# Beginning of a two-layer hybrid backbone: x is loaded first, and half of the first modulation rides move in between the chunks of the first feed-forward layer

## The reference

```python
x = x + _pos_2d(L, x.dtype)[None]
mod_lat = (jax.nn.silu(c) @ w_ada[l] + b_ada[l]).reshape(b, N_MOD, D)     # 9 vectors of 1024
mod_ctx = (jax.nn.silu(c_ctx) @ w_ada[l] + b_ada[l]).reshape(1, N_MOD, D)
# _pre:  rmsnorm(x, g) * (1 + mod[3k+1]) + mod[3k]
# _post: x + weight * mod[3k+2] * rmsnorm(y, g)
x  = _post(x,  _swiglu(_pre(x,  g[0], mod_lat, 0), ffn1_gu[l], ffn1_down[l]), g[1], mod_lat, 0, 0.5)
xc = _post(xc, _swiglu(_pre(xc, g[0], mod_ctx, 0), ffn1_gu[l], ffn1_down[l]), g[1], mod_ctx, 0, 0.5)
```

## Time and profile before

| | us |
|---|---|
| median of 3 runs (lowest, highest) | 2723.16 (2721.18, 2723.31) |
| the profiled execution, its own time | 2723.62 |
| its span in the trace | 2721.8 |
| PE busy in the span | 2630.3 (97%) |
| DVE busy | 1659.4 (61%) |
| ACT busy | 716.5 (26%) |
| POOL busy | 819.7 (30%) |

### The profile page before, as it was taken

The page is one execution under the profiler, slowest core; times in us unless marked ns, Lnnn a source line. Parts: engine busy times, 40 slices in busy tenths (PEclk is TensorE's granted clock), DMA queues, the critical chain, the costliest instruction groups (busy, mean ns, idle before and its releaser), DMA issues.

```text
span 2721.8 us, 41131 instructions
## 1 busy us (share of the span) xinstructions
PE 2630.3 (97%) x17188; PEld 2454.1 (90%) x17188; DVE 1659.4 (61%) x2299; ACT 716.5 (26%) x1016; POOL 819.7 (30%) x1286
## 2 busy tenths in 40 slices
PE   5999999998999999999999999999999999999997
PEld 4999999997969899999999899999999868788886
DVE  5788878767663677667666733443334684644444
ACT  5221221223314321111112422122122414422222
POOL 1268867822130200000000148677551051000001
PEclk9999999999999999999999999999999999999999
DMA  9534544453464143443432232222224456233331
GB/s 330 147 113 159 162 140 135 154 176 120 125 181 141 40 132 111 133 128 119 134 119 86 84 87 84 91 86 91 93 92 141 160 160 188 70 93 101 93 93 62
DMA packets 340465, 337.19 MB, mean 124 GB/s; under 512 B 52528, under 2 KB 311224, under 8 KB 336696
## 3 DMA queue, kind: packets, MB, share of 16 engines
q1 hardware_dynamic: 279224, 204.07, 25.4%
q10 hardware_dynamic: 51840, 77.07, 8.5%
q0 software_dynamic: 9216, 53.42, 5.2%
HBM read 290.02 MB, written 44.50 MB: 123 GB/s over the span
## 4 chain that ended last, share of the span: by engine, by line
PE 86%; DVE 9%; ACT 2%; issue 2%; DMA 1%; SPq 0%; DVEq 0%; ACTq 0%
PE ps L462 78%; PE ps L1619 2%; DVE tmpN L1366 1%; DVE xT L1195 1%; PE ps L1644 1%; DVE tmpN L1389 1%; DVE hL L1393 1%; DMA adaW<-in_w_ada_dram 1%; PE ps L1586 1%; PE ps L1230 1%; ACT wH L447 1%; PE ps L1633 1%; DMA xin<-in_x_dram 1%; PE ps L962 1%; PE ps L981 0%
## 5 line engine op out<-in xcount | busy, mean ns | idle before, releaser
L462 PE MATMUL ps<-hH,wH 128*128 128x384 f32 (+1 forms) x2928 | 1012.3, 346 | 6.5 <-DVE hL L1393 3.8
L462 PE MATMUL ps<-hH,wL 128*128 128x384 f32 (+1 forms) x2928 | 1004.1, 343 | 0.0
L462 PE MATMUL ps<-hL,wH 128*128 128x384 f32 (+1 forms) x2928 | 1003.9, 343 | 0.0
L454 DVE TENSOR_TENSOR wL<-raw,wH 128x1024 fp32r<-128x1024 f32 x300 | 389.4, 1310 | 475.5 <-ACT wH L447 473.9
L462 PEld LDWEIGHTS ps<-hH,wH 128*128 128x128 f32 x2928 | 549.5, 188 | 32.1 <-DVE hL L1393 6.2
L462 PEld LDWEIGHTS ps<-hH,wL 128*128 128x128 f32 x2928 | 549.6, 188 | 18.3
L462 PEld LDWEIGHTS ps<-hL,wH 128*128 128x128 f32 x2928 | 549.7, 188 | 17.9
L462 PE MATMUL ps<-midH,wH 128*128 128x384 f32 (+1 forms) x1232 | 424.7, 345 | 3.7 <-DVE yT L874 3.3
L462 PE MATMUL ps<-midH,wL 128*128 128x384 f32 (+1 forms) x1232 | 422.3, 343 | 0.0
L462 PE MATMUL ps<-midL,wH 128*128 128x384 f32 (+1 forms) x1232 | 422.0, 343 | 0.0
L447 ACT ACTIVATE wH<-raw 128x1024 fp32r<-128x1024 f32 x300 | 310.8, 1050 | 421.7 <-PE ps L462 406.8
(11 more groups left out here) (269 smaller groups left out, 2276.6 us busy)
## 6 DMA issues: line engine op xcount, KB each, us to landing
raw<-in_ffn_gu_dram SPq DMA_DIRECT2D x176, 512.0 KB, 3.8
adaW<-in_w_ada_dram ACTq DMA_DIRECT2D x40, 1536.0 KB, 6.9
raw<-in_ffn_down_dram SPq DMA_DIRECT2D x88, 512.0 KB, 3.5
x_d<-xT POOLq DMA_DIRECT2D x4, 3072.0 KB, 10.3
xT<-x_d POOLq DMA_DIRECT2D x4, 3072.0 KB, 11.4
W_d<-gW POOLq DMA_DIRECT2D x16, 512.0 KB, 3.7
VT_d<-gVT ACTq DMA_DIRECT2D x16, 512.0 KB, 3.0
raw<-in_w_in_dram SPq DMA_DIRECT2D x16, 512.0 KB, 4.3
```

Source lines behind the costliest of these rows:

```text
L454: nc.vector.tensor_tensor(wL[:, n % SPLIT_SLOTS, :], raw[:, n % RAW_SLOTS, :], wH[:, n % SPLIT_SLOTS, :].bitcast(f32), ALU.subtract).then_ ...
L462: ins = nc.tensor.matmul(dst, a, b, start=first and n == 0, stop=last and n == 3 * len(pairs) - 1)
```

## The change

Loads: x is issued first on SP. The parameters are divided between SP's queue and ACT's. POOL issues rides 0 to 4 as soon as the context is there, 5 to 7 when xT is complete. All eight rides have buffers of their own now; lt, lamT, modrow and sq_first lie elsewhere.

Start: DVE takes both parts of each chunk from PSUM (the context copies leave ACT), two chunks ahead of the angle reduction and six behind it; ACT squares each chunk as it comes. PE does ride 0 before the sums of squares and rides 1 to 3 behind them. DVE then goes to the coefficients and `pre_vector` straight after the powers k = 2 to 8 and the three wL; cfR, cfI and P8 (now L2287 to L2306) come behind `pre_vector`, and a new semaphore `s_pow` tells ACT and POOL of them. The coefficients are made in three parts: chunks 0 to 3 after four rides, 4 to 6 after five, 7 after six.

First FFN: `first_groups` takes two units and calls `late_rides` after each chunk, which puts rides 4 to 7 and their turns between the chunks. Unit 2 follows alone, then unit 3 as before. The transfers of rides 8 and 9 are issued by ACT in the middle of `add_shift`.

The core of the diff:

```diff
-    def ada_ride(pe, R, bank, col, between=None):
-        pe.wait_ge(ada_first[R % 6], 16 * (R // 6 + 1))
+    def ada_ride(pe, R, bank, col):
+        pe.wait_ge(ada_first[R], 16)
...
+        def late_ride(R):
+            pe.wait_ge(ada_taken, R - 1)
+            ada_ride(pe, R, 4 + R % 2, 0)
+        def late_rides(place):
+            if place == 0:
+                late_ride(4)
+            elif place == 1:
+                ada_turn(pe, 4, 4, 128)
+                late_ride(5)
+            elif place == 2:
+                ada_turn(pe, 5, 5, 128)
+            elif place == 3:
+                late_ride(6)
+            elif place == 4:
+                ada_turn(pe, 6, 4, 128)
+                late_ride(7)
+            elif place == 5:
+                ada_turn(pe, 7, 5, 128)
+        if F.ride0 == FIRST_RIDES:
+            first_groups(pe, F.base, 2, pre, late_rides)
+            pe.wait_ge(ada_taken, FIRST_RIDES)
+            gate_up(2, 2, None)
+        else:
+            first_groups(pe, F.base, 3, pre)
...
+        if F.ride0 == FIRST_RIDES:          # ffn_scalar, before the first gate
+            act.wait_ge(s_pow, 1)
...
+    LATE_COEFS = {4: (5, 7), 7: (6, 8)}
         for m in range(first, KC):
+            if N.after is None and m in LATE_COEFS:
+                dve.wait_ge(ada_taken, LATE_COEFS[m][0])
+                coef_pre(dve, N, m, LATE_COEFS[m][1])
+                dsync(dve)
...
     def start_sync(sp):
+        sp.dma_start(xin[:, 0:2, :], ctx_in[0]...).then_inc(s_xctx, 16)
+        sp.dma_start(xin[:, 2:6, :], x[0]...).then_inc(s_xin, 16)
+        sp.dma_start(prow[8:16, 4, :], c_ctx...).then_inc(s_par, 16)
...
     def start_pool(pool):
         for R in range(FIRST_RIDES):
-            if R == 2:
-                pool.wait_ge(s_xin, 32)
-            if R >= 6:
-                pool.wait_ge(ada_used, R - 5)
-            pool.dma_start(ada_early[R], ada_source(0, R)).then_inc(ada_first[R % 6], 16)
+            if R == 0:
+                pool.wait_ge(s_xctx, 16)
+            elif R == 5:
+                pool.wait_ge(s_xlat, KC)
+            pool.dma_start(ada_early[R], ada_source(0, R)).then_inc(ada_first[R], 16)
...
     def start_scalar(act):
+        act.dma_start(pdt[...], log_dt...) (two), prow <- lam_re, lam_im, norm_g, c
...
-        for R in range(FIRST_RIDES): ...
+        take_rows(act, 0, 0, 0)
+        split_hi(act, 0)
+        take_rows(act, 1, 1, 0)
+        take_turned(act, 0, 4, 0)
+        split_hi(act, 1)
+        take_rows(act, 2, 2, 0)
+        take_turned(act, 1, 5, 0)
+        split_hi(act, 2)
+        take_rows(act, 3, 3, 0)
+        take_turned(act, 2, 4, 128)
+        take_turned(act, 3, 5, 128)
+        add_shift(act, pres[0], 0, 2)
+        take_rows(act, 4, 4, 0)
+        add_shift(act, pres[0], 2, 3)
+        take_turned(act, 4, 4, 128)
+        take_rows(act, 5, 5, 0)
+        add_shift(act, pres[0], 3, 4)
+        take_turned(act, 5, 5, 128)
+        ada_dma(act, FIRST_RIDES)
+        ada_dma(act, FIRST_RIDES + 1)
...
     def start_vector(dve):
+        for n in range(SPLIT_SLOTS):
+            split_lo(dve, n)
+        dve.wait_ge(s_parT, 3)
+        dve.wait_ge(ada_taken, START_RIDES)
+        coef_pre(dve, pres[0], 0, 4)
+        pre_vector(dve, pres[0])
+        make_fold(dve, FIRST_RIDES)
         lr, li = lamT[:, 0, 0:64], lamT[:, 0, 64:128]      # cfR, cfI, P8: now behind pre_vector
...
-        dlink(dve, tt(P8I[:], lt[:, 14, :], t0, ALU.mult))
-        dsync(dve)
-        for n in range(SPLIT_SLOTS):
-            split_lo(dve, n)
-        dve.wait_ge(s_parT, 3)
-        dve.wait_ge(ada_taken, 2 * KC // RIDE + 1)
-        coef_pre(dve, pres[0])
-        pre_vector(dve, pres[0])
+        tt(P8I[:], lt[:, 14, :], t0, ALU.mult).then_inc(s_pow, 1)
```

More of the change, by code:

```diff
@@ L221, in plink @@
         pool.wait_ge(pool_chain, counts["pool"])
-    ada_first = [sem(f"ada_first{i}") for i in range(6)]
+    ada_first = [sem(f"ada_first{i}") for i in range(8)]
     ada_ready = [sem("ada_ready0"), sem("ada_ready1")]
@@ L477, in wtile, with first_groups @@
         return (wH[:, s, :].rearrange("p (k c) -> p k c", c=cols), wL[:, s, :].rearrange("p (k c) -> p k c", c=cols))
[L479 removed]
+    def first_groups(pe, base, count, pre, between=None):
         pe.wait_ge(w_lo, base + count)
@@ L493, in first_groups @@
                 ins.then_inc(w_used, 1)
+            if between and (u == count - 1 if k < lead else k == KC - 1):
+                between(k if k < lead else lead + u)
     def ffn_sync(sp, F):
@@ L785, in next_ride @@
                 ada_dma(act, R)
-        if F.ride0 is not None:
+        if F.ride0 is not None and F.ride0 != FIRST_RIDES:
             act.wait_ge(h_lo, KC * F.pre.nth + KC)
@@ L2120, in start_tensor @@
         pre_tensor(pe, pres[0])
[L2122 to L2134 removed]
+        ada_ride(pe, 1, 1, 0)
+        ada_turn(pe, 0, 4, 0)
+        pre_spread(pe, pres[0])
+        ada_ride(pe, 2, 2, 0)
+        ada_turn(pe, 1, 5, 0)
+        ada_ride(pe, 3, 3, 0)
+        ada_turn(pe, 2, 4, 128)
+        ada_turn(pe, 3, 5, 128)
+    def start_scalar(act):
+        rows = "l d (q g) p -> (l d q) (g p)"
+        for h in range(2):
+            act.dma_start(pdt[64 * h:64 * h + 64, 0:2], log_dt.rearrange("l d (q g) -> (l d q) g", g=2)).then_inc(s_par, 16)
+        act.dma_start(prow[0:64, 0, :], lam_re.rearrange(rows, g=2)).then_inc(s_par, 16)
+        act.dma_start(prow[64:128, 0, :], lam_im.rearrange(rows, g=2)).then_inc(s_par, 16)
+        act.dma_start(prow[0:96, 1, :], norm_g.rearrange("l i (m p) -> (l i m) p", p=128)).then_inc(s_par, 16)
+        act.dma_start(prow[0:8, 4, :], c.rearrange("a (m p) -> (a m) p", p=128)).then_inc(s_par, 16)
         act.wait_ge(s_par, 16 * 12)
@@ L2142, in start_scalar @@
         nc.scalar.activation(skipD[:].rearrange("p g l q -> p (g l q)"), ps[:, 6, 400:416], ACT.Copy).then_inc(s_parT, 1)
-        for v in range(2):
-            nc.scalar.activation(siluC[:, :, v], ps[:, 6, 384 + 8 * v:392 + 8 * v], ACT.Silu).then_inc(s_silu, 1)
         act.wait_ge(s_lam, 1)
@@ L2147, in start_scalar @@
         nc.scalar.activation(r8[:], lamT[:, 1, 0:64], ACT.Exp, scale=float(T8)).then_inc(s_trig, 1)
+        for v in range(2):
+            nc.scalar.activation(siluC[:, :, v], ps[:, 6, 384 + 8 * v:392 + 8 * v], ACT.Silu).then_inc(s_silu, 1)
         act.wait_ge(s_red, 1)
```

130 lines of the change are left out of this document (54 added, 76 removed).

## The result

| | us |
|---|---|
| the changed kernel, median of 4 runs (lowest, highest) | 2740.24 (2739.3, 2741.04) |
| the kernel before, 4 runs of the same chip | 2722.38 (2721.18, 2723.31) |
| ratio with its 95% interval | 1.0065 [1.0049, 1.0081] |
| the profiled execution: time, span | 2741.04, 2739.2 |

The change makes the kernel 17.9 us slower. The forecast was 2732 with a range of 2722 to 2738. The measured 2740.2 lies outside that range: the forecast was right in sign and in place, and too small by 8 us.

A forecast was written before the change was run, and what follows sets the result against it. PE is 97% busy, but DVE sets its restart at unit 3: X 54.6 + 41.8 + 0.1 = 96.5, plus 1 for the clock, 97.5 against 86.38. That +11, shaded by 2 to +9, gave 2732 us, range 2722 to 2738.

The forecast's parts named there:

- The quantity: PE's restart at unit 3 after waiting for DVE's wL, before at 86.38; its shift moves the whole kernel equally.
- X: Start of the coefficients on DVE, 53.29 before; forecast 54.6, 1.3 later.
- raw 2: Load of unit 2 that ACT's wH waits for; forecast to land at 52, not 40, held beside the rides.
- rival 1: Units not held in the DMA queues: X at 49, restart 90.8, +4.4 to +6.4, time 2729; chance 0.24.
- The gap between rides 4 and 5: Pause of 1.1 to 2.1 us in POOL's ride data, letting 40 to 75 raw packets per engine pass.
- Behind X: DVE's work from X to the restart: +8.8 us, restart at X + 41.8; bounds +7.3 and +10.8.
- a new wait of 1.5: DVE reaches chunk 4 at X + 8.9, ACT's copy for its coefficients comes about X + 10.4: 1.5 us added.
- Gone: the wait for ACT: DVE's earlier wait for ACT behind X disappears, its row and turn copies no longer in front: 1.5 us saved.
- rival 4: PE cold, first two chunks at half clock, ride 4 and chunk 4's coefficients late: restart 100, +14, 2737; chance 0.12.
- The powers: The cfR, cfI and P8 work, 7.5 us, and fold, 0.6, added to DVE between X and unit 3's wL.
- The clock at unit 3: PE idle 4.7 us before the restart instead of 2.0, then low clock: 1 us charged, between 0 and 1.7.
- The shading: 2 us taken off the sum of +11 for queue ends spreading and gaps letting raw pass, giving +9.

The follow-up runs named there:

- e1: Changed kernel with POOL issuing ride 4 only once the first three units have landed; 2730.4 us, ratio 1.0037 to the kernel before.
- e9: Changed kernel with ACT's copies of rides 4 to 7 later, and the turns of rides 5 to 7 later on PE; 2736.5 us.
- e12: e11 with context and x again loaded ahead of parameters and position tables, the rest equal; 2718.7 us.
- e2: Changed kernel with the fold and the cfR, cfI and P8 work moved back ahead of the three wL on DVE; 2729.9 us.
- e4: Changed kernel with the edits of e1 and e2 together; 2727.0 us.
- e3: Changed kernel with 24 small matmuls on PE between unit 2 and unit 3, in its idle time; 2737.2 us.
- e6: e4 plus rides 4 and 5 before the first chunk, later copies of rides 6 and 7, unit 2's high part before ride 3's rows; 2723.6 us.
- e7: Changed kernel with units before ride 4, ride 4 alone before the first chunk, late ACT copies, yT cleared behind unit 3's wL; 2720.6 us.
- e10: Changed kernel with parameters and position tables loaded first, units before ride 4, e9's order, yT cleared behind unit 3's wL; 2718.6 us.
- e11: e10 with 18 small matmuls on PE while it waits for the first chunk; 2716.6 us, ratio 0.9978 to the kernel before.

## Why the prediction came out right in sign and short in size

**The quantity.** The restart at unit 3 moved by 17.86, the span by 17.4, the time by 17.9. The reading of the earlier trace rows, that a later restart is paid in full, holds. That the three numbers agree so closely is luck: 2.1 us of low clock were added right behind the restart, and 2.5 were taken back by other places of low clock later.

**Ahead of X: right, with an error that raw 2 hid.** Raw 2 landed for ACT at 53.07 (forecast 52) and X came at 55.69 (54.6). The rate of one for one, taken from the earlier trace rows at 10 to 14 us, was 612 to 613 at 39 to 47. e1 shows that this is what held X. The rest of the chain was forecast too long: the parameters were there at 17.5 (19), PE turned x at 19.45 (21.3), xT was complete at 30.45 (33), and without the held units X came at 45.83 in e1, where rival 1 has 49. These 3.2 us did not show, since ACT waited for raw 2 anyway; with a smaller hold they would have. The gap between rides 4 and 5, in which 40 to 75 packets of raw per engine were to pass, is the stretch of 33 to 37 us: there SP's queue got 174 packets more than POOL's, 11 per engine.

The Trainium skill ("DMA: Bandwidth & Descriptors", section on queues, rings and completion order) lets an engine take 9 to 17 descriptors of one queue before it turns to the next. With 512-byte rows of units beside 4.5 KB pieces of rides, the trace counts 613 packets of the one for 612 of the other. If a packet of the trace were one descriptor, and only the units took turns of 9 to 17, the units would not have been held; whether the rule reads so, the trace does not show.

**Behind X: the step that failed.** It is the term "Chunk 4's coefficients need ride 4 to have gone through PE, ACT, PE and ACT ... a new wait of 1.5", with "Gone: the wait for ACT". X to the last hL was to grow by 1.3 and grew by 8.33. By e9, 2.2 of the missing 7.0 us are ride 4 itself and 4.8 the order of ACT's copies:

- Ride 4 was turned at X + 12.1, where the forecast has about X + 10. The first chunk ran at half clock and took 4.1 us (59.08 to 63.19) instead of 2.1, ride 4 took 2.48 instead of 1.92. This was in the bounds (+10.8) and was rival 4, which I gave 0.12. e9 shows what it leaves: a wait of 4.08 where the forecast has 1.5. In e12, where the clock is up, ride 4 is turned at X + 9.8 and the wait is 1.84: the term was sized right for the full clock.
- I let ACT's copies for the late rides take their own time only. They stand in ACT's row in front of high parts, which the diff shows (rows of ride 4 between the `add_shift` of chunks 0 and 1 and that of chunk 2), and each waits for PE: with chunk 2's tmpN done by 60.7 ACT stood idle until 65.73 for rows 4, and DVE until 67.75 for chunk 2's high part. The same again at 69.97 and 77.45. e9, which moves these copies and the turns that belong to them and nothing else, gets 4.8 us back. The "wait for ACT" that I counted as gone had become four.

The Trainium skill says that ACT's and DVE's execution queues are strictly in order ("Perfetto Trace Analysis", section on the TensorE instruction). The trace agrees with it by the 4.99 us of idle ACT at 65.73; I used that rule for X and dropped it behind X.

**The powers: right.** 8.1 forecast, 7.93 measured, and e2 confirms that they stand on the path. It was not asked what they cost in front of X; e2 says nothing, as long as raw is late, and e4 says 5.35 once it is not.

**The clock at unit 3.** 1 us charged, 2.1 paid; e3, which keeps the clock up there, confirms the 2.1. PE's idle time was 6.8 where 4.7 were forecast, although PE's own work ended 4.7 later than forecast (97.44, X + 41.75): 2.6 of these are the first chunk and ride 4 at half clock, 1.2 are waits for hL between the chunks.

**The shading.** I took 2 us off a sum of 11 for disorder in the queues. I gave no row for it, and the changed kernel shows it only between 33 and 37 us, worth 11 packets per engine; the shading made the miss larger.

By the runs the 17.9 us are not a sum of separate prices. By the times, taking one term away gives 9.8 (units), 10.3 (powers), 3.8 (ACT's order) or 3.0 (clock, of which 2.1 are its own), and units, powers and rides 4 and 5 together 16.7. These times also hold what later places of low clock add or take. Read 24 matmuls behind unit 3, ahead of those places, the distance to the kernel before is 19.9 us in the changed kernel, 9.3 in e1, 10.3 in e2, 15.4 in e9, 16.8 in e3 and -0.4 in e6. There units, powers and ACT's order taken singly are worth 10.6, 9.6 and 4.5, and the three moves of e6 together 20.3: less than the single values added up, and the whole loss.

## What to carry to other kernels

Before moving work into the gaps of another stage, write down for each engine in the ring what stands behind each waiting instruction: a copy of 0.83 us that waits 5 us for PE costs the engine's whole row 5 us. Two queues that were both full moved equal numbers of packets here (612 and 613), so transfers of 4.5 KB packets held one of 512-byte packets that was needed sooner; let the large ones wait for it, which was worth 10 us (e1). If a stage's row is full, look for what it need not do there (here the clearing of yT, which e7 and e10 to e12 moved together with other things) before moving what it must.

## What was not expected of the hardware

The same idle time of PE was followed by the low clock in one version and not in another. Between 783 and 809 us every version has one of 2.8 to 3.0 us in front of the matmuls on `seqC,PQ`, behind the same instructions. In the kernel before the clock stands at 0.50 for 6.8 us around it and behind it, in nine versions for 3.4 us, and in e2, e4, e7 and e11 not at all. The first row below is the kernel before, the other two are e7:

```profile
788.00:792.00 4.00, 3.33 (x4) 0.50 0.13 16
```
```profile
786.48 1.10 PE L1661 MATMUL ps<-seqC,PQ 128*128 128x512 f32 x2 [2.88 <-DVE hL L2024]
```
```profile
786.00:790.00 4.00, 3.52 (x9) 1.00 0.10 16
```

e7's lead over the kernel before grew there from 2.2 to 5.2 us by this alone. What decides it is not shown; between these versions PE's work at that place is the same and its start differs by up to 25 us. So times that differ by 3 us between versions can be luck of this kind, and the order of e10, e11 and e12 is not shown by their times.
